# Second attention: the meta columns of four heads turned together and weighed in one matmul

## What is computed

```python
kv = (_rmsnorm(ckv, kv_norm_g[l]) @ w_ukv[l]).reshape(B, Tp, MLA_HEADS, QK_NOPE + V_DIM)
s = (einsum('bqhd,bkhd->bhqk', qn, k_nope) + einsum('bqhd,bkd->bhqk', qr, k_rope)) * scale
s = jnp.where(key_pos[None, :] <= q_pos[:, None], s, -1e30)
p = jax.nn.softmax(s, axis=-1)
o = einsum('bhqk,bkhd->bqhd', p, v)
y_att = o @ w_attn_out[l]
```

## Time and profile before

| | us |
|---|---|
| median of three runs (1503.78 to 1504.47) | 1504.22 |
| the profiled execution, its own time | 1505.57 |
| its span, first to last instruction | 1503.7 |
| TensorE busy | 1334.9 |
| VectorE busy | 826.2 |
| ScalarE busy | 421.6 |
| mean granted TensorE clock, share of full speed | 0.985 |

### The profile page before, as it was taken

The page is one execution under the profiler, slowest core; times in us unless marked ns, Lnnn a source line. Parts: engine busy times, 40 slices in busy tenths (PEclk is TensorE's granted clock), DMA queues, the critical chain, the costliest instruction groups (busy, mean ns, idle before and its releaser), DMA issues.

```text
span 1503.7 us, 19261 instructions
## 1 busy us (share of the span) xinstructions
PE 1334.9 (89%) x7372; PEld 884.0 (59%) x7372; DVE 826.2 (55%) x1992; ACT 421.6 (28%) x963; POOL 293.7 (20%) x269
## 2 busy tenths in 40 slices
PE   5999999999999999999999889999877777778776
PEld 2444799998488886888889655454333232323222
DVE  6406667455642344422114387768777777777654
ACT  1203312112153217354102232323322322222212
POOL 0000000000000010000000334446544444444420
PEclk9999999999999999999999899999999999999999
DMA  8343100053321614522244999999999999999995
GB/s 306 107 152 139 44 3 3 1 178 130 124 87 43 210 56 168 165 87 84 99 154 137 412 419 407 408 397 421 421 421 420 422 420 421 421 421 421 421 421 216
DMA packets 65112, 368.03 MB, mean 245 GB/s; under 512 B 7229, under 2 KB 8637, under 8 KB 31933
## 3 DMA queue, kind: packets, MB, share of 16 engines
q0 software_dynamic: 37152, 269.50, 43.3%
q1 hardware_dynamic: 27870, 97.30, 18.8%
HBM read 365.72 MB, written 1.05 MB: 244 GB/s over the span
## 4 chain that ended last, share of the span: by engine, by line
PE 62%; DMA 24%; DVE 10%; ACT 2%; issue 2%; DVEq 0%; POOL 0%; SPq 0%; POOLq 0%; ACTq 0%
DMA arena<-peer_in,arena 19%; PE bank L1600 15%; PE bank L2225 9%; PE bank L432 8%; DMA res<-peer_in,arena 5%; PE bank L1148 3%; PE bank L534 3%; PE bank L2175 3%; DVE arena L2447 2%; PE bank L1228 2%; PE bank L1205 2%; PE bank L1296 2%; PE bank L660 2%; PE bank L2163 1%; PE bank L1684 1%
## 5 line engine op out<-in xcount | busy, mean ns | idle before, releaser
L2225 PE MATMUL bank<-arena 128*128 128x512 f32 x580 | 270.1, 606 | 68.2 <-ACT arena L2316 68.1
L1600 PE MATMUL bank<-arena,ring 128*128 128x256 f32 (+2 forms) x1104 | 234.6, 373 | 4.0 <-DVE arena L2013 1.4
L2225 PEld LDWEIGHTS bank<-arena 128*128 128x128 f32 x580 | 106.8, 192 | 221.3 <-issue 221.1
L1600 PEld LDWEIGHTS bank<-arena,ring 128*128 128x128 f32 x1104 | 199.7, 191 | 33.6 <-DVE cst L1997 2.2
L2447 DVE CUSTOM_DVE_ANT_0 arena<-arena 128x1024 f32<-128x1024 f32 x145 | 175.5, 1222 | 48.7 <-DMA arena<-peer_in,arena 48.7
L2484 POOL DMA_INDIRECT arena<-peer_in,arena x145 | 164.9, 1137 | 175.7 <-PE bank L2225 157.4
L2316 ACT ACTIVATE arena<-cst,arena 128x128 f32<-128x128 f32 x256 | 88.8, 394 | 132.0 <-DVE arena L2397 130.4
L432 PE MATMUL bank<-ring,arena 128*128 128x512 f32 x256 | 114.7, 611 | 8.8 <-DVE arena L847 8.8
L2308 ACT ACTIVATE arena<-arena 128x2 f32<-128x2 f32 x128 | 37.7, 295 | 271.7 <-DVE arena L2447 271.5
L2225 PE MATMUL bank<-ring,arena 128*128 128x512 f32 x176 | 82.9, 610 | 25.0 <-ACT arena L2316 24.9
L432 PEld LDWEIGHTS bank<-ring,arena 128*128 128x128 f32 x256 | 50.0, 196 | 72.4 <-issue 72.4
(11 more groups left out here) (385 smaller groups left out, 1953.1 us busy)
## 6 DMA issues: line engine op xcount, KB each, us to landing
ring<-stream_in SPq DMA_DIRECT2D x160, 512.0 KB, 3.3
ring<-stream_in SPq DMA_DIRECT2D x8, 384.0 KB, 5.5
arena<-peer_in,arena POOLq DMA_INDIRECT x145, 34.2
row<-rows_in SPq DMA_DIRECT2D x4, 512.0 KB, 18.7
cst<-cst_in SPq DMA_DIRECT2D x1, 1929.0 KB, 18.2
res<-res_in SPq DMA_DIRECT2D x2, 544.0 KB, 4.2
row<-rows_in POOLq DMA_DIRECT2D x2, 512.0 KB, 6.5
cst<-rg_w_in SPq DMA_DIRECT2D x1, 1024.0 KB, 8.3
```

Source lines behind the costliest of these rows:

```text
L1600: mm = nc.tensor.matmul(bank[:, first:first + width], slot[:, at + k * cols:at + (k + 1) * cols], src[:, k, :], start=k == 0, stop=k == kt ...
L2225: mm = nc.tensor.matmul(core.banks[2 * t + b][:, :], diag[i % ND], value_half(i, b), start=first, stop=last)
```

## The change

TensorE's sixteen-row work is put together by fours. The 16 meta tokens of the normed `CKV` are repeated eight times to 128 columns (`META`), so that `vm` for n = 0 yields the meta values on all 128 partitions; VectorE evicts them and multiplies by a constant `meta`, which keeps, on 64 rows, for each block of 16 rows one head in four and is zero elsewhere. After the exponentials of every fourth head ScalarE lays the 16 meta columns of four heads side by side (`META_P`), 64 columns, twice, in each half of the queries. TensorE turns the two 128x128 tiles (`turn_meta`), ScalarE keeps them in `PM`, and two matmuls of 128 rows by 256 columns add the meta part of all four heads. The constant adds 8 columns to `cst` and shifts what lies behind it by 32 bytes.

```diff
-    ... ("mask_m", 2 * S),
+    ... ("mask_m", 2 * S), ("meta", 8),
+    put("meta", (i[:, None] < HD) & (i[:, None] // NM == np.arange(8)[None, :] % 4))
@@ TensorE
-                    mm = nc.tensor.matmul(bank[0:count, :], CKV[:, k, at:at + count], slot[:, k * 512:(k + 1) * 512],
-                                          start=k == 0, stop=k == CT - 1)
+                    rows = CKV[:, k, at:at + count] if n else META[:, k * P:(k + 1) * P]
+                    mm = nc.tensor.matmul(bank[:, :], rows, slot[:, k * 512:(k + 1) * 512], start=k == 0, stop=k == CT - 1)
...
-            key = ("pm_c", h // 2)
-            if h % 2 == 0:
-                claim(pe, key, 5)
-            bank = core.banks[core.bank_at[key][0]]
-            for t, at in enumerate((0, KEYS[0])):
-                mm = nc.tensor.transpose(bank[0:NM, (h % 2) * T + t * P:(h % 2) * T + (t + 1) * P], p[:, at:at + NM], cst("ident"))
-            if h % 2:
-                mm.then_inc(*full(key))
+        def turn_meta(n):
+            pe.wait_ge(meta_laid.handle, n + 1)
+            key = ("pm_c", n)
+            bank = claim(pe, key, 5)
+            for t in range(TT):
+                mm = nc.tensor.transpose(bank[:, t * P:(t + 1) * P], META_P[n % 2][:, t * P:(t + 1) * P], cst("ident"))
+            mm.then_inc(*full(key))
...
             if h % 4 == 3:
-                for i in range(h - 3, h + 1):
-                    copied(pe, ("pm_c", i // 2))
-                    pm, vm = PM[:, i % 8 * T:(i % 8 + 1) * T], VM[0:NM, i * HD:(i + 1) * HD]
-                    nc.tensor.matmul(out(i, 0), pm[:, 0:P], vm, start=False, stop=False)
-                    mm = nc.tensor.matmul(out(i, 1), pm[:, P:T], vm, start=False, stop=i == h)
+                n = h // 4
+                copied(pe, ("pm_c", n))
+                for t in range(TT):
+                    mm = nc.tensor.matmul(bank[:, t * T:(t + 1) * T], PM[n][:, t * P:(t + 1) * P], VM[:, n * T:(n + 1) * T],
+                                          start=False, stop=t == TT - 1)
...
+        copied(pe, ("vm", 0, 1))
...
                 turn(i - 2)
+                if i % 4 == 1:
+                    turn_meta((i - 2) // 4)
@@ ScalarE
-            for n in range(3):
+            for n in range(1, 3):
...
+            if h % 4 == 3:
+                n = h // 4
+                act.wait_ge(probs.handle, h + 1)
+                if n >= 2:
+                    filled(act, ("pm_c", n - 2))
+                for t, at in enumerate((0, KEYS[0])):
+                    four = tiles(SC, SW)[:, 4 * n:4 * n + 4, at:at + NM].unsqueeze(1).to_broadcast([P, 2, 4, NM])
+                    ins = nc.scalar.activation(META_P[n % 2][:, t * P:(t + 1) * P].rearrange("p (d h w) -> p d h w", d=2, w=NM), four, ACT.Copy)
+                ins.then_inc(*meta_laid.up())
...
-            if h % 2:
-                bank = filled(act, ("pm_c", h // 2))
-                if h >= 8 and h % 4 == 1:
-                    filled(act, ("o_c", h // 4 - 2))
-                nc.scalar.activation(PM[:, (h - 1) % 8 * T:((h - 1) % 8 + 2) * T], bank[0:NM, :], ACT.Copy)\
-                  .then_inc(*free(("pm_c", h // 2)))
+            if h % 4 == 3:
+                bank = filled(act, ("pm_c", h // 4))
+                nc.scalar.activation(PM[h // 4], bank[:, 0:T], ACT.Copy).then_inc(*free(("pm_c", h // 4)))
@@ VectorE
+        lk(ins)
+        for j in range(CT):
+            ins = nc.vector.tensor_copy(tiles(META[:, j * P:(j + 1) * P], NM), CKV[:, j, 0:NM].unsqueeze(1).to_broadcast([P, P // NM, NM]))
         ins.then_inc(*kv_normed.up())
...
+        for half in range(2):
+            key = ("vm", 0, half)
+            bank = filled(dve, key)
+            by_head = cst("meta").unsqueeze(2).to_broadcast([P, 8, HD])
+            nc.vector.tensor_tensor(tiles(VM[:, half * 512:(half + 1) * 512], HD), tiles(bank[:, :], HD), by_head, ALU.mult)\
+              .then_inc(*free(key))
```

More of the change, by code:

```diff
@@ L80 @@
 CONST_WIDTHS = [
-    ("ident", P), ("ones", P), ("iota", TOPK), ("rope_m", S), ("rope_w", S), ("mask_m", 2 * S),
+    ("ident", P), ("ones", P), ("iota", TOPK), ("rope_m", S), ("rope_w", S), ("mask_m", 2 * S), ("meta", 8),
     ("headones", P), ("rotate", P), ("cum_in", P), ("cum_ex", P), ("carry", 2), ("tri", 3 * P), ("ident_c", HD),
@@ L1553, in second_mix @@
     Y = carve(KT * T)
-    PM = Y[0:NM, :]
+    PM = [Y[:, n * T:(n + 1) * T] for n in range(H // 4)]
+    META = Y[:, H // 4 * T:H // 4 * T + CT * P]
+    META_P = [Y[:, H // 4 * T + CT * P + n * T:H // 4 * T + CT * P + (n + 1) * T] for n in range(2)]
     g.mixed = tiles(Y, T)
@@ L1583, in second_mix @@
     kr_ready, k_ready, q_ready = sig("kr"), sig("k"), sig("q")
-    masked, probs, o_ready = sig("masked"), sig("probs"), sig("o")
+    masked, probs, o_ready, meta_laid = sig("masked"), sig("probs"), sig("o"), sig("meta_laid")
     FILL = list(range(12)) + [13, 15, 17, 18]
@@ L1810, in _ @@
             at = slice(half * 512, (half + 1) * 512)
-            for n in range(3):
+            for n in range(1, 3):
                 bank = filled(act, ("vm", n, half))
-                dst, src = (VM[0:NM, at], bank[0:NM, :]) if n == 0 else (VT[:, (n - 1) * D:n * D][:, at], bank[:, :])
-                nc.scalar.activation(dst, src, ACT.Copy).then_inc(*free(("vm", n, half)))
+                nc.scalar.activation(VT[:, (n - 1) * D:n * D][:, at], bank[:, :], ACT.Copy).then_inc(*free(("vm", n, half)))
         act.wait_ge(lam_in.handle, 1)
```

## The result

| | before | after |
|---|---|---|
| median, us | 1504.0 (1503.36 to 1504.47, 4 runs) | 1492.6 (1491.87 to 1495.62, 4 runs) |
| the profiled execution, its own time | 1505.57 | 1495.62 |
| its span | 1503.7 | 1493.8 |

The ratio is 0.9938, interval 0.9926 to 0.995: 9.3 us faster, 7.5 to 11.1. Forecast were 7.5 us and 1496.7 us with a range from 1495.2 to 1499.9. Executions near 1800 us, with a granted clock of 0.73 to 0.74, are left out of all comparisons; there were two.

The account below looks back on a forecast made before the run. TensorE, busy 89% of the span, was taken to bound the changed stretch. Terms -2.42 - 8.16 + 0.88 + 3.92 = -5.8 us, with -1.7 for the clock's fall -7.5, gave 1504.22 - 7.5 = 1496.7 us, range 1495.2 to 1499.9.

Parts of the forecast that it names:

- (a): Attention on TensorE: meta transposes go, 0.22 us a head; 11 of 16 heads count, 2.42 us gained.
- (c): Attention on TensorE: turn_meta adds two full transposes in iterations 5, 9, 13 and 17, 0.88 us lost.
- (b): Attention on TensorE: four groups of sixteen-row matmuls go, 2.04 us each, 8.16 us gained.
- (d): Attention on TensorE: new wide meta matmuls cost 0.98 us a group, 3.92 us in all, between 3.5 and 4.6.
- (e): Value matmuls: wider meta weight loads, 92 to 190 ns, stay hidden; 0.8 us if each were in the open.
- (f): VectorE behind the kv norm: repeating meta columns delays kv_normed up to 1 us, costing nothing.
- (g): VectorE after the convolution: two masked evictions of meta values, 0.9 us each, fit its idle time and cost nothing.
- (h): ScalarE's exponentials of every fourth head: laying two copies costs 1.0 us a group with the wait, hidden.
- (i): End of attention: last group comes 1.1 us sooner, divide(3) still waits, and the gathers begin earlier by what was saved.
- rival 1: Attention: the clock's fall stays, or was not in the unprofiled runs before; -5.8, 1498.4 us; chance 0.25.
- Rival 3: Gather stage: the 32-byte shift slows transfers; at 33% the time is 1511.7 us; chance 0.03.
- Rival 2: Attention: new waits for ScalarE, or six unlocked heads gain nothing; -4.5, 1499.7 us, or 1498.0 without the fall; chance 0.13.

Follow-up runs that it names:

- e6: Kernel before with the sixteen-row matmuls of all four groups left out; ratio to before 0.9921, attention 91.9 us.
- e2: Kernel before with only the meta values' weights widened from 16 to 128 columns; ratio 0.9998, value matmuls 10.31 us instead of 10.92.
- e4: Kernel before with four more 128x256 matmuls ahead of the attention's first panel; ratio to before 1.0008, attention 105.2 us with two falls.
- e9: Changed kernel with eight 64-column matmuls a group on the first 16 rows only; attention 100.7 us with one fall.
- e1: Kernel before with only the unused 8-column constant added, moving what lies behind it by 32 bytes; ratio 0.9995.
- e5: Changed kernel with each wide meta matmul replaced by four of 64 columns, still on 128 rows; ratio to before 0.9958, attention 97.8 us.
- e10: Changed kernel with VectorE's product that frees bank 2 put ahead of the mask; 1488.99 us, ratio to before 0.9908.

## Why the prediction was right and wrong

**(a), (c), right.** Iteration 3 is 0.22 us shorter, 5 is unchanged, and the even ones from 4 to 10 keep their 5.73 us, with TensorE waiting in place of the removed transposes.

**(b), right, (d), sized 0.12 us too high a group.** The sixteen-row groups were worth 8.2 us without the clock (e6). The new matmuls cost 0.92 with a panel of 3.45 instead of 3.51 behind them, 0.86 net; I had 0.98. That is 0.5 us more gain over four groups.

**A loss that I did not see, 0.35 us.** Iteration 2 grew from 5.73 to 6.08 us. In the changed kernel VectorE starts the product 0.43 us behind the start of the scaling of `mask`, where before it was 0.07 (646.38 and 646.45 us); the 0.26 us of idle time between the two follow on nothing that the profile shows:

```profile
645.15 0.17 DVE L1997 TENSOR_SCALAR small<-small 128x2 f32<-128x2 f32 x1
645.58 0.42 DVE L2018 TENSOR_TENSOR cst<-bank,wide 128x256 f32<-128x256 f32 x1 [0.26 <-issue]
```

All three traces of the changed kernel are 94.2 us long, so it comes each time; its cause stays open. With the 0.5 of (d) it leaves the work's share at 100.1 - 94.2 = 5.9, where I had 5.8.

**(e), the step that failed in mechanism.** I took the 16-column weight loads as hidden, since every matmul there is longer than its load, and noted a possible loss from the wider ones. There was a gain of 0.6 us. The average of 455 ns a record hid it: 24 records at the wide ones' steady distance of 0.43 us make 10.31 us, and 0.6 was lost in the switches between 16 and 128 columns (e2). I had gone by the average and didn't look at the distances one by one.

**(f), (g), (h), (i), right that nothing is added to the path, with prices set too high.** In the rows of the changed kernel the two copies of (f) take 0.36 us, a masked eviction of (g) 0.69 where I had 0.9, with 4.89 us of idle time left behind the second, and the two laid copies of (h) 0.51 together where I had 1.0 with the wait, less than the 0.57 of the copy that went:

```profile
575.63 0.69 DVE L1939 TENSOR_TENSOR arena<-bank,cst 128x512 f32<-128x512 f32 x1 [4.46 <-PE bank L1660]
581.22 0.17 DVE L1943 TENSOR_SCALAR small<-small 128x8 f32<-128x8 f32 x1 [4.89 <-ACT small L1822]
...
652.48 0.51 ACT L1857 ACTIVATE arena<-arena 128x128 f32<-128x128 f32 x2
```

**The clock, right, and better founded now.** The fall went, with its 1.7 us. That it was one fall and not another number is luck as far as the mechanism goes: traces with sixteen-row groups show none, one or two. The prediction named all light work ahead of the fall, narrow matmuls and transposes among it; the runs point to the matmuls on sixteen rows, as far as two traces against one can. The sum by the rule of the Trainium skill (TensorE: Matmul & The Clock Gate, HAM oscillation), by which idle gaps bring the falls, would have left 1.7 us out; here TensorE had no idle time in the 21.3 us ahead of the second fall of e4 and in the 28.7 us ahead of that of e9 (windows of e4 and of e9, granted clock 1.00):

```profile
715.00:736.30 21.30, 21.30 (x141) 19.41 (x140) 3.41 (x15) 6.69 (x17) 0.00 (x0) 1.00 0.20 68
...
700.00:728.70 28.70, 28.70 (x185) 26.21 (x183) 6.30 (x29) 11.24 (x31) 0.00 (x0) 1.00 0.25 86
```

**The sum against its time, the step that missed the range.** Shown by traces are 5.9 for the attention's instructions, 0.6 for the value matmuls and 1.7 for the fall, 8.2 us; the means of the spans differ by 8.5, and both timed ratios hold 8.2 (7.5 to 11.1 and 8.1 to 12.6). The forecast time missed by 4.1 us. Of these, 0.7 are the terms above, 0.6 of it (e), and 0.2 the median of before, which came down to 1504.0. No trace places the other 3.2.

The step that failed is "Against its own time", together with the range: I took 1504.22 us, the median of three runs 0.7 us apart, as the kernel's time, gave no scatter to it or to the median that was to come, and used the 0.7 us against rival 1 too. I had written that 3.0 us is about what a measurement can tell, and put the lower end of the range 1.5 us below the forecast. The runs show the scatter. The 46 timed runs of before in the experiments lie between 1500.8 and 1507.0 us, and four traced ones differ in span from 1497.8 to 1503.7. Attention and code being equal, the first scores come between 633.4 and 636.4 us, by the two falls of the clock ahead of the attention, which come in some executions and not in others, in both kernels; the gather stage takes 676.0 to 678.9, and why it varies isn't shown. About 3 us more on either side would have held the time, by little.

What stays open: the timed ratios give more than the traces in every comparison: 9.3 and 10.4 us against 8.2 for the changed kernel, 6.3 against 4.6 for e5 (4.0 and the 0.6 of the value matmuls), 11.9 against 9.9 for e6, and 13.8 against 12.0 for e10. Each interval holds the smaller number, but all five are off by 1.1 to 2.2 us the same way. A further gain of 1 to 2 us that no trace shows isn't ruled out; one more fall in the attention in the untraced executions of before would be 1.7, and no run tests that.

**The rivals.** Rival 1 (the fall stays, -5.8 us) is out by the traces of the changed kernel, and by the lower end of the measured gain, 7.5 us. Rival 3 (the shift costs) is out by e1. Rival 2 (new waits) came true in small, in iteration 2, but not by ScalarE.

## What to carry to other kernels

Put small matmuls together where the saved instructions lie on TensorE's own chain, and ask of each place what it waits for next: five of the sixteen removed pairs bought nothing until the wait behind them was moved. Average distances of instructions hide the switches between shapes; read the distances at the switch. And a range for the time needs the scatter of whole executions beside the bounds of the edits; three runs close together don't show it.

## What the runs showed of the hardware

- A group of eight 16-row by 64-column matmuls (1.9 us), in unbroken work of TensorE, was followed by a fall of the granted clock to 1.2 GHz 10 times in 36 groups (nine traces); the same work on 128 rows, 64 or 256 columns wide, never in 32 groups (eight traces). Which group is hit differs between executions of the same kernel: the first in three traces of before, the fourth in one. A fall cost 1.7 us.
- Going from 128 to 16 rows and back costs 0.27 us for a group and the panel behind it (e9 against e5, one place), and switching the width of the weights between 16 and 128 columns 0.6 us over the 24 records of the value matmuls.
- An activation that copies 128 strided columns, in pieces of 16, takes 0.30 us, where one that copies 256 contiguous columns takes 0.37 and one of 384 takes 0.47.
